# First attention of a two-block network: weights times values as two products of 64 stationary columns in place of one of 128

## What is computed

```
def one_block(q_blk):
    s = jnp.einsum('bkgqd,bksd->bkgqs', q_blk, kt).astype(jnp.float32) * scale
    p = jax.nn.softmax(s, axis=-1).astype(vt.dtype)
    return jnp.einsum('bkgqs,bksd->bkgqd', p, vt)
```

## Time and profile before

| | |
|---|---|
| median of 2 runs | 2065.02 us (2063.01 to 2067.03) |
| span of the profiled execution | 2060.3 us |
| TensorE busy | 1967.4 us (95%) |
| ScalarE busy | 902.1 us (44%) |
| VectorE busy | 1210.3 us (59%) |
| line 1275 in the first attention | 131.9 us, 256 instructions |
| line 1275 in the two other attentions | 113.5 us, 336 instructions |

### The profile page before, as it was taken

How to read it: one execution, slowest core, us unless ns; L and a number is a source line. 1 busy time by engine, 2 the same in 40 slices (tenths; PEclk the granted TensorE clock), 3 DMA queues, 4 the chain that set the end, 5 groups by cost and what they waited for, 6 DMA issues and landing times.

```text
span 2060.3 us, 23855 instructions
## 1 busy us (share of the span) xinstructions
PE 1967.4 (95%) x8936; PEld 1527.7 (74%) x8936; DVE 1210.3 (59%) x1770; ACT 902.1 (44%) x1486; POOL 93.2 (5%) x172
## 2 busy tenths in 40 slices
PE   4999999999989989999999899999999999999897
PEld 2778876656687768888888688887887876776575
DVE  5686656655585787687555536647434454445645
ACT  4443245555563542333333325424524664445642
POOL 1001100000000000111000000000010000000000
PEclk9999999999999999999999999999999999999998
DMA  9335510010204523445221733344421010003043
GB/s 337 113 103 192 186 52 11 1 52 0 93 1 147 170 92 118 143 170 193 78 70 65 274 119 130 119 158 154 131 100 46 32 42 31 21 21 133 1 174 122
DMA packets 63200, 216.07 MB, mean 105 GB/s; under 512 B 6896, under 2 KB 8048, under 8 KB 62832
## 3 DMA queue, kind: packets, MB, share of 16 engines
q1 hardware_dynamic: 43472, 141.15, 20.2%
q0 software_dynamic: 19616, 73.41, 10.1%
HBM read 177.30 MB, written 34.60 MB: 103 GB/s over the span
## 4 chain that ended last, share of the span: by engine, by line
PE 85%; DVE 7%; ACT 3%; DMA 2%; issue 2%; SPq 1%; POOL 0%; DVEq 0%; ACTq 0%
PE ps L1142 14%; PE ps L1144 14%; PE ps L1143 14%; PE ps L1275 9%; PE ps L1431 6%; PE ps L1433 6%; PE ps L1432 6%; PE ps L1252 3%; PE ps L1253 2%; PE ps L1219 2%; DMA w_raw<-in_weights 1%; PE ps L1234 1%; DMA cmask<-in_consts 1%; SPq L2698 1%; PE ps L1222 1%
## 5 line engine op out<-in xcount | busy, mean ns | idle before, releaser
L1142 PE MATMUL ps<-h_hi,w_hi 128*128 128x512 f32 x832 | 335.8, 404 | 16.7 <-DVE h_lo L2058 10.1
L1144 PE MATMUL ps<-h_hi,w_lo 128*128 128x512 f32 x832 | 326.1, 392 | 0.0
L1143 PE MATMUL ps<-h_lo,w_hi 128*128 128x512 f32 x832 | 325.9, 392 | 0.0
L2021 DVE TENSOR_TENSOR w_lo<-w_raw,w_hi 128x1024 fp32r<-128x1024 f32 x139 | 170.0, 1224 | 251.1 <-ACT w_hi L1565 249.7
L1565 ACT ACTIVATE w_hi<-w_raw 128x1024 fp32r<-128x1024 f32 x140 | 147.7, 1056 | 264.2 <-DMA w_raw<-in_weights 262.4
L2149 DVE TENSOR_REDUCE mh<-ps 128x1 f32<-128x512 f32 x192 | 124.7, 654 | 147.6 <-PE ps L1219 70.7
L1142 PEld LDWEIGHTS ps<-h_hi,w_hi 128*128 128x128 f32 x832 | 157.8, 190 | 54.7 <-issue 12.0
L1144 PEld LDWEIGHTS ps<-h_hi,w_lo 128*128 128x128 f32 x832 | 157.1, 189 | 34.1
L1143 PEld LDWEIGHTS ps<-h_lo,w_hi 128*128 128x128 f32 x832 | 157.7, 189 | 31.6 <-issue 1.4
L1142 PE MATMUL ps<-hid_hi,w_hi 128*128 128x512 f32 x352 | 139.3, 396 | 6.8 <-DVE hid_late_lo L2021 2.9
L1431 PE MATMUL ps<-t_hi,pair_S_r 128*128 128x512 f32 x352 | 137.8, 391 | 3.5 <-DVE pair_S_r L2021 2.6
(11 more groups left out here) (384 smaller groups left out, 3849.7 us busy)
## 6 DMA issues: line engine op xcount, KB each, us to landing
w_raw<-in_weights SPq DMA_DIRECT2D x140, 512.0 KB, 3.6
ada_next<-in_ada POOLq DMA_DIRECT2D x32, 512.0 KB, 4.6
ada_last<-in_ada POOLq DMA_DIRECT2D x24, 512.0 KB, 5.5
pair_gate<-in_weights SPq DMA_DIRECT2D x22, 512.0 KB, 3.7
pair_up<-in_weights SPq DMA_DIRECT2D x22, 512.0 KB, 4.7
ada_first<-in_ada SPq DMA_DIRECT2D x8, 1024.0 KB, 14.9
m_scratch<-y POOLq DMA_DIRECT2D x12, 512.0 KB, 5.0
hid_scratch<-hid_out POOLq DMA_DIRECT2D x22, 256.0 KB, 2.3
```

The costliest lines, as they stand in the source:

```text
L1142: e.matmul(o, w_hi[slot][:, tile_of(kw)], hi, start=start, stop=False, skip_group_check=skip)
L1143: e.matmul(o, w_hi[slot][:, tile_of(kw)], lo, start=False, stop=False, skip_group_check=skip)
L1144: return e.matmul(o, w_lo[slot][:, tile_of(kw)], hi, start=False, stop=stop, skip_group_check=skip)
L2021: return e.tensor_tensor(dst, src, hi.bitcast(F32), ALU.subtract)
```

## The change

In the first attention alone ("full"), the values product is cut in two by its stationary columns: columns 0 to 63 (the values) into partitions 0 to 63, then columns 64 to 127 (the ones) into partitions 64 to 127, both with the same moving operand. "band" and "fox" keep the one product of 128 columns.

```
                 for kt, q0, q1, c in columns_of(kind, h, n, u):
                     o = ps[:, bank, q0 - n * HT:q1 - n * HT]
-                    x = e.matmul(o, A.v[kb][:, kt, :], A.pf[p3][:, c:c + q1 - q0], start=(u == 0 and kind != "band"), stop=False,
-                                 skip_group_check=True)
+                    first = u == 0 and kind != "band"
+                    for r in (0, 64) if kind == "full" else (0,):
+                        wide = slice(r, r + 64) if kind == "full" else slice(0, P)
+                        x = e.matmul(o[wide, :], A.v[kb][:, kt, wide], A.pf[p3][:, c:c + q1 - q0], start=first, stop=False,
+                                     skip_group_check=True)
                 x.then_inc(s["val"], 1)
```

## The result

The changed kernel takes 2108.09 us in the median of two runs (2106.24 to 2109.94), 1.0214 times the kernel before, interval 1.0188 to 1.0241: 43 us slower. Timed again beside the kernel before on one chip it took 2105.79 against 2062.42 us, 1.0208 (1.0179 to 1.0236). The prediction was 2177 us with a range from 2116 to 2228. The sign was right, and the time lies under the range.

A forecast was written before the change was run, and what follows sets the result against it. TensorE was taken to bound the kernel. Third pass 55.0, weights of the ones 6.4 and change of form 50.8 us made 112 us on 2065, so 2177 us, range 2116 to 2228.

The forecast's parts named there:

- What bounds the kernel: First attention: TensorE bounds it, so its stream's changes move the end one for one; at most 4.1 us soaked up.
- A pass of 64 columns is as long as one of 128: Split values product: a float32 pass with 64 stationary columns takes 0.43 us, as the whole product's pass does.
- The order decides, so that there are three lengths: Split pair: queue order lets only the middle two of four passes overlap, three lengths for two, +0.43 us a unit.
- Ones pass 1: First of the ones product's two float32 passes, third in program order; said to run beside the values product's second pass.
- the third pass: Split pair in the first attention: one more pass length a unit, 128 x 0.43 = 55.0 us.
- the weights of the ones: Split pair: loading the ones' weights before their first pass adds 0.05 us a unit, 128 x 0.05 = 6.4 us.
- the second form of D: Split pair: products run wholly side by side but the form costs 0.40 us a round trip; 2116 us, chance 0.05.
- The change of form: Between whole-array products and split pairs: 0.20 us each way, 127 x 0.40 = 50.8 us.
- (iii): Trace sign: the pair's first load starts some 0.3 us behind the last whole-array matmul if the form costs, else at once.
- (i): Trace sign: the ones' first pass starts 0.05 us behind the values' second if they overlap, 0.43 if not.
- (ii): Trace sign: length of a unit with a line 1219 product, 2.43 us by the forecast's sum, other lengths for rivals.
- A: Rival, split pair: overlap and no cost of the form, 55 to 61 us more, 2120 to 2127 us; chance 0.20.

The follow-up runs named there:

- experiments 2: The changed kernel without the values product in seven of each job's eight units, ones product kept: 2103.54 us, 1.0194 times the kernel before.
- 4: First attention's scores, helper row, maxima and values all float32 and split into column halves, against the same products whole: 2315.85 against 2296.47 us.
- Experiments 3: The split kernel with two units' values steps put together, for fewer form changes, against whole products in the same order: 2091.76 against 2072.42 us.

## Why the prediction was wrong

**What bounds the kernel: right.** TensorE bounds the stage, and what was added to its stream moved the end one for one: +107 us for a third product on a used half, where 0.86 us at 128 units makes 110. The prediction allowed for at most 4.1 us soaked up by TensorE's idle time, and about 3 were.

**A pass of 64 columns is as long as one of 128: right.** 0.43 us, to the digit (experiments 2 and 4).

**The order decides, so that there are three lengths: wrong, and this is the step that failed.** "Ones pass 1 is behind it in the queue and can run beside values pass 2" took the queue for strictly in order. It isn't, between halves. Ones pass 1 overtook values pass 2 and ran beside values pass 1. The terms that hung on it, 55.0 us for the third pass and 6.4 us for the weights of the ones, are both zero: the pair takes two lengths and not three. Of the 112 us forecast, 61 were for something that cost nothing, and the sign came out right by the term of the form alone. The prediction had the case as the second form of D, 2116 us, with a chance of 0.05. What it held against it, "matmul starts in the trace keep the program's order", came from a trace with no two matmuls on different halves. Such a trace can't show an overtaking of this kind. The rows bore out that order was kept among matmuls that share the array's columns, and I carried it to matmuls that don't.

**The change of form: the mechanism right, the size a little high.** I took 0.20 us each way from the split by rows, 50.8 us at 127 places. The split by columns has 0.15 going in and 0.20 coming out. At 127 places that makes 44 us; the stage grew by 39, for the reasons given above, and the median by 43. Experiments 3 and 4 show that it is the form: 19 us for half as many changes, and nothing inside a stage of one form. The Trainium skill's page TensorEngine Tiling (Array Packing), section Key Properties, says that changing the tiling mode drains TensorE and changing the tile does not; the traces agree with both halves of it. Its other rule there, that different tiles can run loads and matmuls in parallel, says nothing of an order between them; the prediction's third length came from the order that it added. By the rule alone the pair takes 0.86 us and not 1.29, and it took 0.86 beside the 0.15 of the form.

**Signs and marks.** Of the marks set for the trace, (iii) came as said: the first load of the pair starts some 0.3 us behind the last whole-array matmul (335.50 against a start at 335.18 us), after an idle time of 0.36 us in the mean (45.2 us at 127 places). (i) and (ii) told at once that the case was none of those named as likely: ones pass 1 starts ahead of values pass 2, and a unit of 1.92 us lies under 1.98, A's.

**The range.** The prediction calls its lower end, 2116, A's, but A's own sum starts at 2120; 2116 is the second form of D, overlap in full with 0.40 us a round trip. (Its chances for "slower" add up to 0.94 too, where it has 0.92.) The rows gave the price of a round trip between 0 and 0.40, so with the halves side by side anything from 2065 to 2116 was open, and I had weighed only the ends.

## What to carry to other kernels

In these runs, cutting a float32 product by its stationary columns into halves of the array was free on TensorE as long as its neighbours were cut too, and cost about a third of a microsecond a time when whole-array products stood before and behind it; so put split products next to each other. Two products on different halves ran side by side even when one stood two or four passes behind in the program. With eight passes of one half first, the other half started 0.49 us late: write them in turn. In this kernel the second half did nothing new, so only the price was left; a use that puts two different moving operands on the two halves wasn't tried.

## What the runs showed of the hardware that was not expected

- A matmul on one half of the array's columns starts ahead of matmuls on the other half that stand before it in the program: two of them start in the same 0.1 us, where the program has two passes of one half first. With eight passes ahead, it went past the last three, 0.49 us into the unit; with four ahead it went past three at once (2105.62 us, the changed kernel's time).
- Passes on one half stay one behind the other: six passes, four of them on one half, took 1.87 us, 4 x 0.43 + 0.15.
- Going from the whole array to halves by columns costs 0.15 us, going back 0.20 us, both with 512 moving columns behind or ahead; from a product of 33 rows to halves by columns and back to the whole costs 0.15 us more than from it to the whole.
